# Combinations of x made earlier, one head's end of norm cut into eight pieces, another's moved forward

## The chip, the cores and the metric

The kernel runs on one core of a Trainium2 chip. The metric is the device time of one execution in microseconds. One core has five engines with a queue each: TensorE (PE, matmuls), VectorE (DVE), ScalarE (ACT), GpSimd (POOL) and SyncE (SP, which here only starts DMAs). Each engine works through its queue in order, and semaphores tie the queues together.

## The reference

One layer of a hybrid encoder, on 2048 new frames and 64 frames of a running stream. The core of it:

```python
p = rms_norm(x, norm_g) @ w_in            # aq, ak, av, ag, bq, bf, bi, bg, ma, mb
attn_o = window_attention(aq, ak, av)     # mixer A: window of two chunks of 64
# mixer B, for each chunk of 64 and each of 4 heads:
o = scores @ v + q_dec @ S                # read-out
S = exp(last) * S + k_end.T @ v           # update of the state
ya = (attn_o * silu(ag)) @ w_ba
rn = rec_o * rsqrt(mean(rec_o * rec_o) + EPS) * g_norm
yb = (rn * silu(bg)) @ w_bb
y = rms_norm(x + (sigmoid(ma) * ya + sigmoid(mb) * yb) @ w_o)
```

All arithmetic is to be as exact as float32: each matrix product is done in three passes over operands split into a high and a low part.

## The kernel before

The 2112 frames are cut into three groups of 704 columns (11 chunks of 64); each group runs the same stages. Within a group a projection of 128 output rows is two half blocks on PE, a first half of 320 columns and a second of 384, 24 matmuls each. `steps(g)` writes the order of one group as a list of steps, and each engine walks the same list and does its own part of each step. So a step's place in the list is its place in the queue of every engine that has a part in it. The order of a group:

- k, v and q of mixer A, then the projections of the four heads of mixer B (`bf`, `bq`, `bi`, `bg`), with attention in between. Behind each head's projections its recurrence runs beside the next head's; head 3's runs beside the gates of mixer A, `ag0` to `ag3`: `kend_t`, `v_t`, `scores_b` (masked scores, first half of ag1), `update` (second half of ag1), `read_out` (second half of ag2), `sum_sq` (second half of ag3).
- `update` on DVE (line 1204) adds the chunks' states one after the other and signals `last_made`; `read_out` on PE (line 1567 on) waits for it. ScalarE copies the read-out to `ob` and squares it, DVE makes the low part `sq_lo` (line 1226), PE sums the squares.
- `finish` (from line 1227, DVE alone) is the end of a head's norm: a reciprocal of 704 columns, two multiplications, a copy to the high part and a subtraction for the low part. ScalarE may copy the next head's read-out to `ob` only when it is done. Its signal `finished` is wanted by ScalarE's copy of the first product of the fourth pair, and by PE's `yb`.
- Most merge gates (`ma`, `mb`; 14 of 16 blocks) are computed in pairs by Strassen's scheme in Winograd's form: seven half-size products (`prod`, of 12 matmuls with 352 columns) instead of eight. That needs combinations of the two row halves and the two column halves of x. GpSimd makes two of the sums (line 650), `t_mix` on DVE two more sums and four differences, `t_high` (ScalarE) and `t_low` (DVE) split them, `t_last` and `t_low` 3 the last one, `t_one`, which is written over a quarter of x once the last full projection is through.
- The weights are combined too, in group 0 alone: `prep` makes the high part (ScalarE, line 701) and the sums (DVE, lines 1270 to 1283), `low` the low part (DVE, line 1046). Three of eight weight buffers hold the raw blocks of a pair (DMA, line 550), five are a ring for what is made. All that is made is kept in DRAM (`w_parts`, line 683) and groups 1 and 2 load it from there. A buffer may be made anew when PE has used it and its copy to DRAM has landed.
- In the products, line 1295 on DVE adds the products to each other out of their banks and frees these banks; line 929 on ScalarE copies the first one (`u_sum`), line 787 is ScalarE's sigmoid of the full gate projections.
- Then `ya`, `yb` (mixer outputs), `out` (output projection), norm of y, and x of the next group.

These lines of `steps` are the ones that the change touches:

```python
        if n == 4:
            out.append(("finish", B_HEADS - 2, 0))
    out.append(("t_mix", 0, 0))
...
        out += {1: [("t_high", 0, 0)], 2: [("t_high", 1, 0), ("t_high", 2, 0), ("t_low", 0, 0)]}.get(n, [])
        if n == 2 * len(firsts) - 2:
            out += prep(2, 3) + [("t_low", 1, 0), ("t_low", 2, 0)]
    out += [("t_last", 0, 0), ("prod", 0, 0)] + prep(4) + [("t_low", 3, 0), ("finish", B_HEADS - 1, 0)]
```

Of the kernel before, what the change touches and what calls it, by code (L numbers as in the profile page):

```python
# [12 lines left out]
F32 = mybir.dt.float32  # L13
# [4 lines left out]
ALU = mybir.AluOpType  # L18
# [16 lines left out]
B_HEADS = 4  # L35
# [4 lines left out]
T = NCH * CHUNK  # L40
# [113 lines left out]
def steps(g):  # L154

    last, out = g == GROUPS - 1, []

    def block(n):

        return [(kind, n, s) for s in range(2) for kind in ("proj", "evac")]  # L160


    hgrn = [["kend_t0", "kend_t1"], ["v_t0", "v_t1"], ["scores_b0", "scores_b1"], ["update0"],
            [], ["read_out0", "read_out1"], [], ["sum_sq0", "sum_sq1"]]

    def recurrence(n, h):
        return [(k[:-1], h, int(k[-1])) for k in hgrn[n]] if h >= 0 else []


    out += [(kind, n, s) for s in range(2) for n in ("ak", "av", "bf0") for kind in ("proj", "evac")]  # L170
    if g:
        out[4:4] = [("y_sum", 1, g - 1)]
        out[7:7] = [("y_back", 1, g - 1)]
    for n in ["aq0", "aq1"]:
        out += block(n)
    out += [("v_win", r, 0) for r in range(3)] + [("k_win", 0, 0)]
    for n in ["aq2", "aq3"]:
        out += block(n)
    heads = [(f"{n}{h}", s) for h in range(B_HEADS) for n in ("bf", "bq", "bi", "bg") for s in range(2)]
    for n, half in list(enumerate(heads))[2:]:  # L180


        h, i, k = n // 8, n % 8, (n - 2) // 2
        out.append(("proj", *half))
        chunk = [("attend", k - 2, 0)] if n % 2 else [("probs_t", k - 2, 0), ("scores", k, 0)]
        parts = [[t for t in chunk if 0 <= t[1] < NCH], [("evac", *half)], recurrence(i, h - 1)]
        order = {0: (2, 0, 1), 3: (0, 1, 2)}.get(i, (0, 2, 1))
        out += [t for j in order for t in parts[j]]
        if n % 2 == 0:
            out += [(kind, c, 0) for kind, c in (("softmax", k), ("normalise", k - 1)) if 0 <= c < NCH]  # L190
        if i == 4:
            out.append(("keys", h, 0))
        if i == 0 and h >= 2:
            out.append(("finish", h - 2, 0))
    gates = [(f"ag{j}", s) for j in range(A_GROUP) for s in range(2)]
    for n, half in enumerate(gates):

        parts = [("evac", *half)], recurrence(n, B_HEADS - 1)
        out += [("proj", *half)] + (parts[1] + parts[0] if n == 1 else parts[0] + parts[1])
        if n == 4:  # L200
            out.append(("finish", B_HEADS - 2, 0))
    out.append(("t_mix", 0, 0))

    def prep(*ops):
        return [("prep", n, 0) for n in ops if g == 0 and n < NO]

    firsts = PLAIN[NP - 2 * FIRST_PAIRS:]
    for n, half in enumerate((m, s) for m in firsts for s in range(2)):
        out += [("proj", *half), ("evac", *half)]
        if n == 2 * len(firsts) - 4:  # L210
            out += prep(0, 1)
        out += {1: [("t_high", 0, 0)], 2: [("t_high", 1, 0), ("t_high", 2, 0), ("t_low", 0, 0)]}.get(n, [])
        if n == 2 * len(firsts) - 2:
            out += prep(2, 3) + [("t_low", 1, 0), ("t_low", 2, 0)]
    out += [("t_last", 0, 0), ("prod", 0, 0)] + prep(4) + [("t_low", 3, 0), ("finish", B_HEADS - 1, 0)]
    for n in range(1, NO):
        out += ([("prod", n, 0)] + prep(n + AHEAD))[::1 if OPS[n][0] == "a11" else -1]
        out += {NO - 3: [("fetch", 0, 0)], NO - 1: [("fetch", 1, 0), ("refill", 0, 0)]}.get(n, [])
    for j in range(MERGES):
        out += [(n, j, s) for n in ("ya", "yb") for s in range(2)]  # L220
    for n, (j, s) in enumerate(OUT):
        if not last:
            out += X_STEPS.get(n, [])
        out.append(("out", j, s))
        if (j, s) == (KT - 3, 1):
            out += [("y_sum", 0, g), ("y_back", 0, g)]
    if last:
        out += [("y_sum", 1, g), ("y_back", 1, g)]
    if g == 0:
        out = [t for step in out for t in [step] + [("low", u, 0) for u in lows_after(step)]]  # L230
    return out
# [37 lines left out]
def program(nc, x_t, w, cache_k, cache_v, state, norm_gain, sinks, lb_logits, hgrn_gain, final_gain,  # L269
# [26 lines left out]
    gb_hi, at_gb_hi, _ = sb("gb_hi", [P, B_HEADS, T], F32R)  # L296
    ga_lo, at_ga_lo, _ = sb("ga_lo", [P, NCH, A_GROUP, CHUNK], F32R)
    gb_lo, at_gb_lo, _ = sb("gb_lo", [P, B_HEADS, T], F32R)
# [3 lines left out]
    gate_b = own("gate_b", [P, B_HEADS, T], F32, at_gb_lo)  # L302
# [3 lines left out]
    for h in range(HALVES):  # L306
# [15 lines left out]
    gain, gain_b = own("gain", [P, KT]), own("gain_b", [P, B_HEADS])  # L322
# [14 lines left out]
    f, at_f, _ = sb("f", [P, T + 1])  # L337
    prod = own("prod", [P, T])
    sq, at_sq, _ = sb("sq", [P, T])
    sq_lo = own("sq_lo", [P, T], F32R, at_sq)  # L340
    sq_hi, rs, ob = own("sq_hi", [P, T], F32R), own("rs", [P, T]), own("ob", [P, T])
    t_one = own("t_one", [P, 4, HT], F32, at_f)
# [28 lines left out]
    t_top = own("t_top", [P, 3, 4, HT], F32, at_t_hi)  # L371
    t_sum = own("t_sum", [P, 3, 4, HT], F32, at_t_lo)
# [25 lines left out]
    t_back, t_made, t_high, t_split, t_one_low = (sem("t_back"), sem("t_made"), sem("t_high"), sem("t_split"),  # L398
                                                  sem("t_one_low"))
# [3 lines left out]
    ob_copied, finished, gated_a = sem("ob_copied"), sem("finished"), sem("gated_a")  # L403
# [21 lines left out]
    def wait_read(eng, g, last, step, b):  # L425

        eng.wait_ge(read[b], START + use(g, last, step, b) + 1)

    def wait_block_read(eng, g, last, name):

        halves = [("proj", name, s) for s in range(2)]
        if bank_of(g, halves[0]) != bank_of(g, halves[1]):
            wait_read(eng, g, last, halves[0], bank_of(g, halves[0]))
        wait_read(eng, g, last, halves[1], bank_of(g, halves[1]))
# [531 lines left out]
    def _(dve):  # L966
        links = [0]

        def link(ins):

            links[0] += 1
            ins.then_inc(dve_step, 1)
            dve.wait_ge(dve_step, links[0])
# [74 lines left out]
        def split(hi, lo, val):  # L1048

            link(dve.tensor_copy(hi, val))  # L1050
            return dve.tensor_tensor(lo, val, hi.bitcast(F32), ALU.subtract)
# [18 lines left out]
        def body(g, last):  # L1070
            dve.sem_clear(dve_step)
            links[0] = 0
            for step in steps(g):
                kind, a, s = step
                if kind == "evac":
# [4 lines left out]
                    n = a[:2]  # L1080
# [17 lines left out]
                    elif n == "bf" and s == 1:  # L1098
                        h = int(a[2:])
# [10 lines left out]
                    elif n == "bq":  # L1110
                        h = int(a[2:])
                        wait_full(dve, g, last, step, bank)
                        dve.tensor_tensor(q_dec[:, h, lo:hi], src, prod[:, lo:hi], ALU.mult).then_inc(read[bank], 1)
                    elif n == "bg":
                        h = int(a[2:])
# [15 lines left out]
                elif kind == "keys":  # L1131

                    h = a
# [10 lines left out]
                elif kind == "scores":  # L1144
# [11 lines left out]
                    for b in (3, 4):  # L1156
# [5 lines left out]
                                                  in1=neg_sink[:], op0=ALU.mult, op1=ALU.min))  # L1162
# [9 lines left out]
                elif kind == "scores_b":  # L1172
                    h, b = a, banks(step)[0]
# [16 lines left out]
                elif kind == "update":  # L1190

                    h = a
# [5 lines left out]
                    for c in range(NCH):  # L1198
                        b = UPDATE_BANK[c]
                        i = UPDATE_BANKS[b].index(c)  # L1200
                        if i == 0:
# [3 lines left out]
                            out=dst, in0=st[:, c, :], scalar=decay[:, h, c:c + 1],  # L1205
                            in1=pb[b][:, i * P:(i + 1) * P], op0=ALU.mult, op1=ALU.add)
# [20 lines left out]
                elif kind == "finish":  # L1227
                    h = a
# [6 lines left out]
                                                  op0=ALU.mult, op1=ALU.mult))  # L1235
                    link(dve.tensor_tensor(ob[:], ob[:], gate_b[:, h, :], ALU.mult))
                    split(gb_hi[:, h, :], gb_lo[:, h, :], ob[:]).then_inc(finished, 1)
                elif kind == "t_mix":

                    def back(dst, k, t):  # L1240

                        v = slice(4 * k, 4 * k + 4), slice(HT * t, HT * t + HT)
                        return dve.tensor_tensor(dst, x_hi[:, v[0], v[1]].bitcast(F32),
                                                 x_lo[:, v[0], v[1]].bitcast(F32), ALU.add)

                    dve.wait_ge(t_back, 2 * g + 2)
                    back(t_sum[:, 1], 1, 0)
                    link(back(t_top[:, 1], 0, 0))
                    dve.tensor_tensor(t_one[:], t_top[:, 0], t_top[:, 1], ALU.subtract).then_inc(t_made, 1)
                    dve.tensor_tensor(t_sum[:, 0], t_sum[:, 2], t_top[:, 0], ALU.subtract).then_inc(t_made, 1)  # L1250
                    dve.wait_ge(t_made, 4 * g + 2)
                    dve.tensor_tensor(t_sum[:, 2], t_sum[:, 2], t_one[:], ALU.subtract).then_inc(t_made, 1)
                    dve.wait_ge(t_made, 4 * g + 3)
                    dve.tensor_tensor(t_sum[:, 1], t_sum[:, 1], t_sum[:, 2], ALU.subtract).then_inc(t_made, 1)
                elif kind == "t_low" and a == 3:
                    dve.wait_ge(t_high, 4 * g + 4)
                    dve.tensor_tensor(x_lo[:, 0:4, HT:T], t_one[:], x_hi[:, 0:4, HT:T].bitcast(F32),
# [5 lines left out]
                elif kind == "prep" and OPS[a][0] == "s3":  # L1263

                    n, at = a, PAIRS * g + OPS[a][1]
# [6 lines left out]
                elif kind == "prep" and OPS[a][0] == "s2":  # L1272
                    n, at = a, PAIRS * g + OPS[a][1]
# [61 lines left out]
                elif kind == "out":  # L1335
                    n = OUT.index((a, s))
# [362 lines left out]
```

## Time and profile before

| | us |
|---|---|
| median of three runs | 1567.97 |
| lowest and highest run | 1567.23, 1568.9 |
| profiled execution | 1567.78 |
| its span, first to last instruction | 1565.7 |
| group 0: first product | 308 |
| groups 1 and 2: head 3's read-out | 802.50, 1303.07 |

The mean granted clock of TensorE is 0.992 of full speed. The profile gives for each engine its instructions with start and duration in microseconds from the start of the span, and in brackets how long the engine stood idle before one and what ended that. Matmuls overlap in the rows, so their pace is read from start to start. Group 0 lasts until about 527 us, group 1 until about 1030.

### The profile page before, as it was taken

Reading aid. Unit: us, or ns where it says so; the run is one execution under the profiler, and the core shown is the slowest. Engines: PE = TensorE matmul, PEld = TensorE weight load, DVE = VectorE, ACT = ScalarE, POOL = GpSimd, SP = SyncE. Lnnn points to the kernel's source line nnn. Section 1 sums busy time; section 2 is a strip of 40 time slices with the busy share of each in tenths; the row PEclk is TensorE's granted clock in tenths of the full one; section 3 lists DMA queues with packets and bytes.
Section 4 is the critical chain, followed back from the end, with each engine's and each line's share of the span. In section 5 each row is a group of like instructions: output and inputs, shape, how many; then the busy total and the mean of one; then the engine's idle time right before and its main releaser. Section 6 shows DMA issues by size and latency. Waiting matters only on the chain.

```text
span 1565.7 us, 24417 instructions
## 1 busy us (share of the span) xinstructions
PE 1513.8 (97%) x9727; PEld 1459.3 (93%) x9727; DVE 967.2 (62%) x1658; ACT 552.4 (35%) x1193; POOL 40.0 (3%) x24
## 2 busy tenths in 40 slices
PE   6999999889999999999999999999999999999996
PEld 5998899888999999999999999999989999999996
DVE  5677877986676854677686136665566668414624
ACT  5355553434415522565222120531246423210022
POOL 2000001000001000000100000100000010000000
PEclk9999999999999999999999999999999999999998
DMA  4743344368896663222237884545332233886452
GB/s 158 281 169 125 136 151 158 124 251 305 322 329 231 229 233 117 108 85 96 100 112 229 275 291 172 209 145 202 111 112 82 85 112 111 270 273 203 138 200 74
DMA packets 99136, 278.44 MB, mean 178 GB/s; under 512 B 11984, under 2 KB 29136, under 8 KB 99024
## 3 DMA queue, kind: packets, MB, share of 16 engines
q1 hardware_dynamic: 73968, 202.68, 37.9%
q10 hardware_dynamic: 25056, 74.20, 12.2%
q8 instruction: 78, 1.28, 0.3%
q14 instruction: 34, 0.28, 0.1%
HBM read 194.01 MB, written 82.84 MB: 177 GB/s over the span
## 4 chain that ended last, share of the span: by engine, by line
PE 79%; DVE 11%; DMA 4%; ACT 3%; issue 2%; SPq 1%; ACTq 0%; DVEq 0%
PE bank L1366 23%; PE bank L1368 23%; PE bank L1367 23%; DMA w_parts<-w_unit 2%; PE bank L1571 2%; PE bank L1497 1%; DVE rs L1233 1%; PE bank L1567 1%; DMA raw<-in_w 1%; PE bank L1515 1%; DVE w_unit L1046 1%; PE bank L1529 1%; PE bank L1553 1%; PE bank L1539 1%; PE bank L1506 1%
## 5 line engine op out<-in xcount | busy, mean ns | idle before, releaser
L1366 PE MATMUL bank<-x_hi,w_unit 128*128 128x320 f32 (+2 forms) x1680 | 554.0, 330 | 22.0 <-DVE sig L1295 8.1
L1368 PE MATMUL bank<-x_hi,w_unit 128*128 128x320 f32 (+2 forms) x1680 | 543.6, 324 | 0.0
L1367 PE MATMUL bank<-x_lo,w_unit 128*128 128x320 f32 (+2 forms) x1680 | 543.3, 323 | 0.0
L1366 PEld LDWEIGHTS bank<-x_hi,w_unit 128*128 128x128 f32 x1680 | 317.3, 189 | 33.1 <-issue 18.8
L1367 PEld LDWEIGHTS bank<-x_lo,w_unit 128*128 128x128 f32 x1680 | 317.5, 189 | 0.4
L1368 PEld LDWEIGHTS bank<-x_hi,w_unit 128*128 128x128 f32 x1680 | 317.4, 189 | 0.0
L1366 PE MATMUL bank<-m_hi,w_unit 128*128 128x384 f32 (+1 forms) x384 | 125.7, 327 | 1.1 <-DVE w_unit L1046 1.1
L1368 PE MATMUL bank<-m_hi,w_unit 128*128 128x384 f32 (+1 forms) x384 | 123.8, 322 | 0.0
L1367 PE MATMUL bank<-m_lo,w_unit 128*128 128x384 f32 (+1 forms) x384 | 123.8, 322 | 0.0
L1366 PE MATMUL bank<-t_hi,w_unit 128*128 128x352 f32 x252 | 81.5, 324 | 0.0
L1367 PE MATMUL bank<-t_lo,w_unit 128*128 128x352 f32 x252 | 81.5, 323 | 0.0
L1368 PE MATMUL bank<-t_hi,w_unit 128*128 128x352 f32 x252 | 81.5, 323 | 0.0
L938 ACT ACTIVATE sig<-sig 128x352 f32<-128x352 f32 x63 | 31.1, 494 | 139.9 <-DVE sig L1295 139.9
L1046 DVE TENSOR_TENSOR w_unit<-w_raw,w_unit 128x512 fp32r<-128x512 f32 x96 | 65.0, 686 | 17.5 <-ACT w_unit L691 12.7
L1366 PEld LDWEIGHTS bank<-m_hi,w_unit 128*128 128x128 f32 x384 | 72.1, 188 | 2.2 <-issue 1.5
L1367 PEld LDWEIGHTS bank<-m_lo,w_unit 128*128 128x128 f32 x384 | 72.1, 188 | 0.7
L1368 PEld LDWEIGHTS bank<-m_hi,w_unit 128*128 128x128 f32 x384 | 72.1, 188 | 0.0
L691 ACT ACTIVATE w_unit<-w_raw 128x512 fp32r<-128x512 f32 x88 | 51.2, 624 | 47.3 <-DMA w_raw<-in_w 44.0
L1295 DVE TENSOR_TENSOR u_sum<-u_sum,bank 128x352 f32<-128x352 f32 x21 | 10.9, 520 | 90.1 <-PE bank L1368 90.1
L1342 DVE TENSOR_TENSOR res<-res,bank 128x320 f32<-128x320 f32 (+1 forms) x48 | 24.9, 518 | 65.5 <-PE bank L1368 62.4
L1366 PE MATMUL bank<-ga_hi,w_unit 128*128 128x320 f32 (+1 forms) x192 | 61.9, 323 | 0.9 <-DVE sig L1330 0.9
L1366 PE MATMUL bank<-gb_hi,w_unit 128*128 128x320 f32 (+1 forms) x192 | 62.0, 323 | 0.2 <-DVE sig L1330 0.2
(209 smaller groups left out, 2464.9 us busy)
## 6 DMA issues: line engine op xcount, KB each, us to landing
w_unit<-w_parts SPq DMA_DIRECT2D x274, 512.0 KB, 4.1
w_parts<-w_unit ACTq DMA_DIRECT2D x137, 512.0 KB, 4.3
w_raw<-in_w SPq DMA_DIRECT2D x88, 256.0 KB, 3.6
res<-in_x_t SPq DMA_DIRECT2D x12, 704.0 KB, 6.9
raw<-in_w SPq DMA_DIRECT2D x28, 256.0 KB, 5.4
x_raw<-in_x_t SPq DMA_DIRECT2D x12, 384.0 KB, 7.4
out_y<-res SPq DMA_DIRECT2D x12, 384.0 KB, 6.2
x_raw<-in_x_t SPq DMA_DIRECT2D x12, 320.0 KB, 5.6
```

The source lines that it names most:

```text
L691: act.activation(high_of(u), w_raw[PLACE[u]][:], ACT.Copy).then_inc(w_high, 1)
L938: act.activation(v, v, ACT.Sigmoid).then_inc(gates_made, 1)
L1046: dve.tensor_tensor(low_of(u), source, high_of(u).bitcast(F32), ALU.subtract).then_inc(w_split, 1)
L1233: link(dve.reciprocal(rs[:], rs[:]))
L1342: dve.tensor_tensor(r, r, pb[bank][:, 0:hi - lo], ALU.add).then_inc(read[bank], 1)
L1366: pe.matmul(out, w_h, m_h, start=first, stop=False, **more)
L1367: pe.matmul(out, w_h, m_l, start=False, stop=False, **more)
L1368: return pe.matmul(out, w_l, m_h, start=False, stop=last_of_bank, **more)
L1497: ins = pe.matmul(pb[3 + v][:, i * P:(i + 1) * P], q_rot[rows, c, 2 * i:2 * i + 2, :], k_rot[rows, c * CHUNK:c * CHUNK + P], start=True, s ...
L1506: ins = pe.transpose(pb[5][:, i * P:(i + 1) * P], probs[:, a % 2, i, :], ident[:])
L1515: ins = pe.matmul(pb[6][rows, 0:2 * P], v_win[:, a, rows], probs_t[:, 2 * v:2 * v + 2, :], start=True, stop=True)
L1571: ins = pe.matmul(pb[b][:, k * CHUNK:(k + 1) * CHUNK], st[:, c, :], q_dec[:, a, c * CHUNK:(c + 1) * CHUNK], start=False, stop=(c == chunks ...
```

## The change

- `t_mix` is cut into three steps. The first (two sums) comes behind head 3's first `bg` half, the second (two differences) behind its second half, the third (two more) behind the first half of ag0. Before, all six instructions came behind the last ag block.
- `finish` of head 2 moves from behind the first half of ag2 to behind the first half of ag1, behind `scores_b` and ahead of `update`.
- `t_high` 0 to 2 move into the last three ag halves; `t_low` 0 comes behind the first half of ma0, `t_low` 1 and 2 behind its second.
- `finish` of head 3 no longer comes in one piece behind the first product and `t_low` 3, but in eight (`finish_part`): four quarters of the reciprocal behind products 4, 6, 8 and 10, the two multiplications behind 12 and 14, the copy behind 16, the subtraction with the signal behind 18. The waits stand at the first piece.

```diff
--- before.py
+++ after.py
@@ -192,14 +192,19 @@
             out.append(("keys", h, 0))
         if i == 0 and h >= 2:
             out.append(("finish", h - 2, 0))
+        if h == B_HEADS - 1 and i in (6, 7):
+            out.append(("t_mix", i - 6, 0))
     gates = [(f"ag{j}", s) for j in range(A_GROUP) for s in range(2)]
     for n, half in enumerate(gates):
 
         parts = [("evac", *half)], recurrence(n, B_HEADS - 1)
         out += [("proj", *half)] + (parts[1] + parts[0] if n == 1 else parts[0] + parts[1])
-        if n == 4:
+        if n == 2:
             out.append(("finish", B_HEADS - 2, 0))
-    out.append(("t_mix", 0, 0))
+        if n == 0:
+            out.append(("t_mix", 2, 0))
+        if n >= 5:
+            out.append(("t_high", n - 5, 0))
 
     def prep(*ops):
         return [("prep", n, 0) for n in ops if g == 0 and n < NO]
@@ -209,12 +214,14 @@
         out += [("proj", *half), ("evac", *half)]
         if n == 2 * len(firsts) - 4:
             out += prep(0, 1)
-        out += {1: [("t_high", 0, 0)], 2: [("t_high", 1, 0), ("t_high", 2, 0), ("t_low", 0, 0)]}.get(n, [])
+        out += {0: [("t_low", 0, 0)], 1: [("t_low", 1, 0), ("t_low", 2, 0)]}.get(n, [])
         if n == 2 * len(firsts) - 2:
-            out += prep(2, 3) + [("t_low", 1, 0), ("t_low", 2, 0)]
-    out += [("t_last", 0, 0), ("prod", 0, 0)] + prep(4) + [("t_low", 3, 0), ("finish", B_HEADS - 1, 0)]
+            out += prep(2, 3)
+    out += [("t_last", 0, 0), ("prod", 0, 0)] + prep(4) + [("t_low", 3, 0)]
     for n in range(1, NO):
         out += ([("prod", n, 0)] + prep(n + AHEAD))[::1 if OPS[n][0] == "a11" else -1]
+        if n >= 4 and n % 2 == 0 and n < 20:
+            out.append(("finish_part", B_HEADS - 1, n // 2 - 2))
         out += {NO - 3: [("fetch", 0, 0)], NO - 1: [("fetch", 1, 0), ("refill", 0, 0)]}.get(n, [])
     for j in range(MERGES):
         out += [(n, j, s) for n in ("ya", "yb") for s in range(2)]
@@ -1235,6 +1242,25 @@
                                                   op0=ALU.mult, op1=ALU.mult))
                     link(dve.tensor_tensor(ob[:], ob[:], gate_b[:, h, :], ALU.mult))
                     split(gb_hi[:, h, :], gb_lo[:, h, :], ob[:]).then_inc(finished, 1)
+                elif kind == "finish_part":
+                    h, quarter = a, slice(T // 4 * (s % 4), T // 4 * (s % 4 + 1))
+                    if s == 0:
+                        wait_read(dve, g, last, ("sum_sq", h, 0), 7)
+                        wait_read(dve, g, last, ("sum_sq", h, 1), 5)
+                        dve.wait_ge(ob_copied, 2 * (B_HEADS * g + h + 1))
+                        wait_block_read(dve, g, last, f"bg{h}")
+                    if s < 4:
+                        link(dve.reciprocal(rs[:, quarter], rs[:, quarter]))
+                    elif s == 4:
+                        link(dve.scalar_tensor_tensor(out=ob[:], in0=ob[:], scalar=gain_b[:, h:h + 1], in1=rs[:],
+                                                      op0=ALU.mult, op1=ALU.mult))
+                    elif s == 5:
+                        link(dve.tensor_tensor(ob[:], ob[:], gate_b[:, h, :], ALU.mult))
+                    elif s == 6:
+                        link(dve.tensor_copy(gb_hi[:, h, :], ob[:]))
+                    else:
+                        dve.tensor_tensor(gb_lo[:, h, :], ob[:], gb_hi[:, h, :].bitcast(F32),
+                                          ALU.subtract).then_inc(finished, 1)
                 elif kind == "t_mix":
 
                     def back(dst, k, t):
@@ -1243,15 +1269,18 @@
                         return dve.tensor_tensor(dst, x_hi[:, v[0], v[1]].bitcast(F32),
                                                  x_lo[:, v[0], v[1]].bitcast(F32), ALU.add)
 
-                    dve.wait_ge(t_back, 2 * g + 2)
-                    back(t_sum[:, 1], 1, 0)
-                    link(back(t_top[:, 1], 0, 0))
-                    dve.tensor_tensor(t_one[:], t_top[:, 0], t_top[:, 1], ALU.subtract).then_inc(t_made, 1)
-                    dve.tensor_tensor(t_sum[:, 0], t_sum[:, 2], t_top[:, 0], ALU.subtract).then_inc(t_made, 1)
-                    dve.wait_ge(t_made, 4 * g + 2)
-                    dve.tensor_tensor(t_sum[:, 2], t_sum[:, 2], t_one[:], ALU.subtract).then_inc(t_made, 1)
-                    dve.wait_ge(t_made, 4 * g + 3)
-                    dve.tensor_tensor(t_sum[:, 1], t_sum[:, 1], t_sum[:, 2], ALU.subtract).then_inc(t_made, 1)
+                    if a == 0:
+                        dve.wait_ge(t_back, 2 * g + 2)
+                        back(t_sum[:, 1], 1, 0)
+                        link(back(t_top[:, 1], 0, 0))
+                    elif a == 1:
+                        dve.tensor_tensor(t_one[:], t_top[:, 0], t_top[:, 1], ALU.subtract).then_inc(t_made, 1)
+                        dve.tensor_tensor(t_sum[:, 0], t_sum[:, 2], t_top[:, 0], ALU.subtract).then_inc(t_made, 1)
+                    else:
+                        dve.wait_ge(t_made, 4 * g + 2)
+                        dve.tensor_tensor(t_sum[:, 2], t_sum[:, 2], t_one[:], ALU.subtract).then_inc(t_made, 1)
+                        dve.wait_ge(t_made, 4 * g + 3)
+                        dve.tensor_tensor(t_sum[:, 1], t_sum[:, 1], t_sum[:, 2], ALU.subtract).then_inc(t_made, 1)
                 elif kind == "t_low" and a == 3:
                     dve.wait_ge(t_high, 4 * g + 4)
                     dve.tensor_tensor(x_lo[:, 0:4, HT:T], t_one[:], x_hi[:, 0:4, HT:T].bitcast(F32),
```

## Rows read from the trace of the kernel before

**Rows 1.** The page, part 1: busy time, share of the span, number of instructions

```profile
PE 1513.8 (97%) x9727; PEld 1459.3 (93%) x9727; DVE 967.2 (62%) x1658; ACT 552.4 (35%) x1193; POOL 40.0 (3%) x24
```

**Rows 2.** Waits of PE, whole span: total us, times, longest us

```profile
PE bank L1366 <- DVE sig L1295: 8.1, 7, 2.0
...
PE bank L1366 <- ACT sig L787: 0.7, 1, 0.7
```

**Rows 3.** Timeline of DVE, group 1: start, duration, engine, line, [idle before <-releaser]

```profile
777.63 0.56 DVE L1117 TENSOR_TENSOR gate_b<-bank,gate_b 128x384 f32<-128x384 f32 x1 [6.50 <-ACT gate_b L821]
...
788.00 0.49 DVE L1124 TENSOR_TENSOR raw<-bank,raw 128x320 f32<-128x320 f32 x1 [0.74 <-ACT raw L829]
...
790.01 0.06 DVE L1182 MEMSET pad<- 128x1 f32 x1
...
793.81 0.56 DVE L1124 TENSOR_TENSOR raw<-bank,raw 128x384 f32<-128x384 f32 x1 [2.47 <-ACT raw L829]
...
795.87 0.22 DVE L1197 COPY st<-carry_s 128x128 f32<-128x128 f32 x1
...
800.56 0.35 DVE L1204 SCALAR_TENSOR_TENSOR carry_s<-st,decay,bank 128x128 f32<-128x128 f32 x1
...
803.03 4.55 DVE L1233 RECIPROCAL rs<-rs 128x704 f32<-128x704 f32 x1
...
810.90 0.55 DVE L1124 TENSOR_TENSOR raw<-bank,raw 128x384 f32<-128x384 f32 x1
...
821.54 1.62 DVE L1249 TENSOR_TENSOR t_one<-t_top 128x1408 f32<-128x1408 f32 x1
...
824.74 1.62 DVE L1252 TENSOR_TENSOR t_sum<-t_sum,t_one 128x1408 f32<-128x1408 f32 x1
```

**Rows 4.** Timeline of PE, group 1, head 3's read-out

```profile
802.50 1.05 PE L1567 MATMUL bank<-sc_t,v_tok 128*128 128x128 f32 x8
```

**Rows 5.** Timelines of DVE and of PE, group 0, around head 3's read-out

```profile
254.24 0.68 DVE L1046 TENSOR_TENSOR w_unit<-w_raw,w_unit 128x512 fp32r<-128x512 f32 x1
...
277.29 0.35 DVE L1204 SCALAR_TENSOR_TENSOR carry_s<-st,decay,bank 128x128 f32<-128x128 f32 x1
...
278.64 0.61 PE L1567 MATMUL bank<-sc_t,v_tok 128*128 128x128 f32 x4
...
291.82 0.50 PE L1582 MATMUL bank<-sq_hi,ones_r 128*128 128x512 f32 x1 [1.22 <-DVE sq_lo L1226]
```

**Rows 6.** Timeline of GpSimd (POOL), group 1

```profile
763.78 3.17 POOL L650 TENSOR_TENSOR t_top<-x_hi,x_lo 128x1408 f32<-128x1408 f32 x1
```

**Rows 7.** Timeline of PE, group 0, at the first products

```profile
313.87 0.40 PE L1366 MATMUL bank<-x_hi,w_unit 128*128 128x352 f32 x1 [3.76 <-ACT u_sum L929]
...
327.62 0.43 PE L1366 MATMUL bank<-x_hi,w_unit 128*128 128x352 f32 x1 [4.27 <-DVE w_unit L1046]
```

**Rows 8.** Stretches: length, busy PE, PEld, DVE, ACT, POOL; clock, DMA share, GB/s

```profile
314.00:318.00 4.00, 4.00 (x16) 4.00 (x17) 3.76 (x6) 0.93 (x2) 0.00 (x0) 0.57 0.02 4
...
378.00:383.00 5.00, 4.01 (x15) 4.04 (x16) 3.85 (x7) 1.89 (x4) 0.00 (x0) 0.66 0.65 260
383.00:398.00 15.00, 15.00 (x95) 15.00 (x94) 9.80 (x17) 6.17 (x12) 0.00 (x0) 1.00 0.85 316
833.00:930.00 97.00, 95.65 (x598) 95.14 (x597) 28.79 (x45) 16.96 (x35) 0.00 (x0) 1.00 0.84 272
```

**Rows 9.** One line by source: count, duration ns min/median/max

```profile
L1168 DVE RECIPROCAL rden<-rden x33: 177/178/180, 98.0 to 1237.4; 128x4 f32<-128x4 f32 x33
```

**Rows 10.** Timeline of DMA issues (SPq), and one piece of the chain, group 0

```profile
316.99 0.33 SPq L550 DMA_DIRECT2D raw<-in_w  x1
...
337.29 0.33 SPq L550 DMA_DIRECT2D raw<-in_w  x1
...
398.41 0.33 SPq L550 DMA_DIRECT2D raw<-in_w  x1
...
340.95 5.62 DMA w_parts<-w_unit
```

## The prediction

> **What bounds the kernel now.** I read the page first. TensorE (PE) is busy for 97% of the span, VectorE (DVE) for 62% [rows 1]. So time can only come out of PE's idle microseconds, or go into new ones. Next, the list of PE's waits: seven waits, 8.1 us, end with DVE's adds of line 1295, the longest 2.0 us; one of 0.7 us ends with line 787 [rows 2]. PE's timeline has two longer ones, 3.76 and 4.27 us, in group 0 close behind the start of the products [rows 7]. Groups 1 and 2 hold almost no waits. So only group 0 has anything large to give back.
>
> A wait of PE costs more than itself. Behind the one of 3.76 us PE starts 16 matmuls in 4 us at a granted clock of 0.57; elsewhere it starts 95 in 15 us at 1.00, one in 0.16 us [rows 8]. A granted clock of 0.57 is full speed (2.4 GHz) for a small part of the stretch and 1.2 GHz for the rest. 16 matmuls are worth 2.6 us, so 1.4 are lost, and by the clock (0.43 x 4) 1.7. I take 1.6. After the wait of 2.0 us, at 378 to 383 us, the clock is 0.66: the loss is the same.
>
> Then I read the queue of DVE, which works in order, from the last head's gate on. In group 1 it waits 6.50, 0.74 and 2.47 us among the gate blocks, then runs the update of head 3 until 800.91 [rows 3]. PE starts head 3's read-out at 802.50 [rows 4] and needs that update: 1.6 us to spare. In group 0 the update ends at 277.64 and the read-out starts at 278.64 [rows 5]: 1.0 us. This is the tight place, and the change puts work ahead of it.
>
> **Part 1: the combinations (t_mix) go forward.** The six instructions on 128x1408 stand in three pairs of 3.20 us from start to start (821.54 to 824.74) [rows 3]. The first pair now falls behind the gate of head 3's first half, inside the idle time of 6.50 us that begins at 771.1: free. GpSimd's two adds, for which it waits, end at 766.95 [rows 6]. The second pair stands behind the gate of the second half, which ends at 778.19, the third behind the first half of ag0: 6.4 us ahead of the update.
>
> **Part 2: head 2's end of norm** goes from behind the first half of ag2 to behind the first half of ag1, which is from behind the update to ahead of it. It takes 7.87 us (803.03 to 810.90) [rows 3]. Queued behind it are the second half of ag1 and the update, and so PE's read-out with every matmul after it.
>
> **The sum ahead of the read-out.** In group 1 DVE must do from 778.19 on, from start to start in rows 3: second pair 3.20, first half of ag0 2.01 (as 788.00 to 790.01), third pair 3.20, second half of ag0 2.06 (793.81 to 795.87), first half of ag1 2.01, masked scores 1.34 (790.01 to 791.34, where the wait of 2.47 begins), end of norm 7.87, second half of ag1 2.06, update 5.04 (795.87 to 800.91). That is 28.8 us, and all of it is ready when DVE gets there, so it ends at 807.0 against 802.5: PE waits **4.5 us**. Group 2 repeats these rows within 0.1 us: 4.5. In group 0 the start is 254.85 (0.61 behind 254.24) and four low parts of weights of 0.61 lie between: 31.2 us, so 286.0 against 278.64 [rows 5], **7.4 us**. Each is longer than 2.0 us, so 1.6 us for the clock go on each. Bounds of that: 0 (no row shows these short matmuls at the low clock) and 1.7; I take 1.6, since all waits of 2.0 us and more cost it.
>
> Given back: with its norm done early, head 2 no longer holds up ScalarE's copy of head 3's read-out, and PE's wait of 1.22 us for sq_lo goes in group 0 [rows 5]. In groups 1 and 2 PE did not wait there.
>
> **Part 3: t_high and t_low sooner.** They fit between the gate blocks on ScalarE, and behind them on DVE. That takes away the 0.7 us of group 1 at line 787 [rows 2], behind a ScalarE still busy with t_high. Of the 3.76 us in group 0 about 1.1 stay: the copy of t_one's high part must wait for the last full projection, and the first product's copy stands behind it.
>
> **Part 4: head 3's end of norm in eight pieces.** Before, these 7.87 us stood ahead of the low part for which PE waits 4.27 us [rows 7]. Now the pieces stand behind products 4, 6, ... 18. A quarter of the reciprocal is 4.55/4 = 1.14 us and a fixed part; a reciprocal of 4 elements takes 0.18 [rows 9], so about 1.3, and the other four are the old 3.3 us. In groups 1 and 2 DVE works 28.8 of 97 us there [rows 8], so they are free; without that cover they would cost up to 8.5 us. The Trainium skill (VectorE: DVE Perf Modes, "The TRN2 errata") speaks against cutting an instruction up, as each part pays a fixed latency again. The row of 4 elements agrees; it is 0.45 us for a reciprocal in four here, and is held in the sum already.
>
> **What comes next in group 0's products.** There a ring of five buffers sets the pace: each made weight is first written to DRAM, which takes up to 5.62 us, before its buffer is made anew. The raw weights of a pair are fetched when the last sum of the pair before is made. The fetches are issued at 316.99, 337.29, then 15.28 us apart on average until 398.41 [rows 10], while seven products take PE 7 x 12 x 0.16 = 13.4 us. So the change saves what it moves this chain forward against PE. The first product starts 12 x 0.16 us ahead of the wait of 3.76, at 308.1 [rows 7]; relative to it the fetches stood at 8.9, 29.2 and 90.3. Afterwards the first can come once the last full projection frees the ring, at 3.9: a copy, a low part and three sums of 0.6 to 0.8 us, with their waits. The second comes 15.3 later plus 2.0 for two pieces that stand directly between a low part and the sums of the next pair: 21.2. The last stands at 21.2 + 61.1 = 82.3. That is 8.0 us earlier, less 0.3 for later pieces: **7.7 us** won. Bounds: 2 (all the pieces lie in the chain) and 17 (the chain never binds: all waits but 1.1 go, 3.76 + 4.27 + the 6.7 of line 1295's 8.1 us that lie in group 0, and 3.2 of lowered clock).
>
> **Total.** Group 0: 7.4 + 1.6 - 1.2 - 7.7 = +0.1. Group 1: 4.5 + 1.6 - 0.7 = +5.4. Group 2: 4.5 + 1.6 = +6.1. Sum +11.6. The profiled execution took 1567.8 us (span 1565.7), 0.2 under the median of the runs, so 1579.4 in all.
>
> **The rivals.**
> *A, the forecast*: the update is late in all three groups, 1579.4. For it speaks that the durations repeat from group to group and that nothing in that queue waits.
> *B, the weak form*: the stalls come, but the clock stays up behind them (-4.8) and the chain gives 11 instead of 7.7: 1571.3. Or the clock falls and all 17 us come back: 1570.1, the border to no change. For it: the wait of 1.22 us cost no more than itself. Against: 2.0 us and more did. The Trainium skill (TensorE: Matmul & The Clock Gate, Part 1) ties the clock to recent activity; by that rule all three stalls would lower it, as in A.
> *C, faster*: head 2's end of norm fits ahead of the update after all. The point that decides is whether DVE ends the update before PE is through the second half of ag2, that is whether 28.8 us of work shrink to 24.3 in group 1, and 31.2 to 23.8 in group 0. Then only gains stay, 1.2 + 0.7 + 7.7: 1558.2. The steadiness of the rows speaks against it.
> *D, the pieces cost more*: all of them lengthen group 0's chain, 5.7 us more: 1585.1. For it: DVE works 9.8 of 15 us there [rows 8], and each piece stands directly ahead of a low part or a sum.
> *E, it does not come sooner*: the first pair waits for GpSimd, and all behind it slips. GpSimd is done 4.2 us before [rows 6]; only what it is late beyond that counts. It ends slower too.
>
> **How the numbers follow.** A 0.70, B 0.12, C 0.06, D 0.10, E 0.02. The range is 1571 (B) to 1585 (D); it leaves out C and the edge of B. Two measurements of this kernel tell apart about 0.2%, 3.1 us. Faster by more: C and a little, 0.07. Within: the edge of B, 0.06. Slower: the rest, 0.87.
>
> **What would show it.** Right: PE idle 4 to 5 us ahead of line 1567 at the last head of groups 1 and 2 and 6 to 7 in group 0, ended by DVE's line 1204; DVE without a gap from head 3's gate to the end of the update; a granted clock under 0.7 right behind; the wait of 4.27 us gone and 1 us left of the 3.76; the fetches of raw weights about 8 us earlier relative to the first product; no wait for sq_lo. Wrong: gaps in DVE's queue ahead of the update, no wait at line 1567, or more waits at the products of group 0 than before. The dearest error would be in the sum ahead of the read-out, since it enters three times.

## The result, and the profile after

| | before | changed |
|---|---|---|
| median of four runs, us | 1568.08 | 1591.49 |
| lowest and highest | 1567.23, 1568.9 | 1589.92, 1593.45 |
| profiled execution, us | 1567.78 | 1591.22 |
| its span, us | 1565.7 | 1589.2 |
| mean granted clock | 0.992 | 0.982 |

The ratio is 1.015, with a 95% interval of 1.0132 to 1.0168: 23.4 us slower. The forecast was 1579.4, 11.6 us slower, with a range that ended at 1585, so the measured time lies beyond it. The direction was right, the size only half.

The page of the changed kernel, part 1, against [rows 1]:

```profile
PE 1527.6 (96%) x9727; PEld 1472.7 (93%) x9727; DVE 967.0 (61%) x1667; ACT 552.8 (35%) x1193; POOL 40.1 (3%) x24
```

PE is busy for 13.8 us more than before with the same 9727 matmuls, so they ran longer. That is already a sign that waits are not all. PE's waits, whole span (against [rows 2]; line 1596 is the old 1567, line 1324 the old 1295):

```profile
PE bank L1596 <- DVEq L1224: 14.4, 3, 6.1
PE bank L1395 <- DVE sig L1324: 10.9, 9, 2.8
...
PE bank L1395 <- ACT u_sum L936: 2.2, 3, 0.9
PE bank L1582 <- DVE sc_t L1195: 1.5, 2, 1.1
```

There is one new entry: three waits, 14.4 us in all, at the first matmul of head 3's read-out. The profile puts them down to line 1224 of DVE's queue, the signal behind the update. They are 6.06 us in group 0 and 4.19 in groups 1 and 2. DVE's timeline of group 1, against [rows 3]:

```profile
783.41 0.56 DVE L1124 TENSOR_TENSOR gate_b<-bank,gate_b 128x384 f32<-128x384 f32 x1 [3.50 <-ACT gate_b L828]
783.89 1.61 DVE L1277 TENSOR_TENSOR t_one<-t_top 128x1408 f32<-128x1408 f32 x1
...
786.95 0.48 DVE L1131 TENSOR_TENSOR raw<-bank,raw 128x320 f32<-128x320 f32 x1
...
797.42 4.54 DVE L1240 RECIPROCAL rs<-rs 128x704 f32<-128x704 f32 x1
...
805.28 0.55 DVE L1131 TENSOR_TENSOR raw<-bank,raw 128x384 f32<-128x384 f32 x1
...
807.33 0.22 DVE L1204 COPY st<-carry_s 128x128 f32<-128x128 f32 x1
...
812.02 0.35 DVE L1211 SCALAR_TENSOR_TENSOR carry_s<-st,decay,bank 128x128 f32<-128x128 f32 x1
...
822.05 0.89 DVE L1233 TENSOR_TENSOR sq_lo<-sq,sq_hi 128x704 fp32r<-128x704 f32 x1 [5.42 <-ACT sq_hi L906]
```

After 3.50 us of idle time nothing in this queue waits until the last row: second pair of combinations, first half of ag0, third pair, the next two halves, end of norm from 797.42, second half of ag1 from 805.28, update from 807.33 to 812.37. That is 28.4 us behind the gate (783.97). The sum of 28.8 holds. PE's timeline right behind, against [rows 4]:

```profile
812.57 2.05 PE L1596 MATMUL bank<-sc_t,v_tok 128*128 128x128 f32 x8 [4.19 <-DVEq L1224]
...
820.30 0.61 PE L1395 MATMUL bank<-x_hi,w_unit 128*128 128x320 f32 x1
820.71 0.47 PE L1396 MATMUL bank<-x_lo,w_unit 128*128 128x320 f32 x1
...
823.91 0.47 PE L1396 MATMUL bank<-x_lo,w_unit 128*128 128x320 f32 x1
...
824.41 0.31 PE L1395 MATMUL bank<-x_hi,w_unit 128*128 128x320 f32 x1
...
846.79 0.40 PE L1395 MATMUL bank<-x_hi,w_unit 128*128 128x352 f32 x1 [0.67 <-ACT sig L794]
```

The last of these rows is the first product. In the kernel before it stands here:

```profile
831.49 0.40 PE L1366 MATMUL bank<-x_hi,w_unit 128*128 128x352 f32 x1 [0.67 <-ACT sig L787]
```

And the stretches around it, with the columns of [rows 8]: length, busy PE, PEld, DVE, ACT, POOL, then the granted clock, DMA share, GB/s:

```profile
812.00:816.00 4.00, 3.43 (x16) 3.46 (x17) 3.67 (x8) 0.00 (x0) 0.00 (x0) 0.50 0.21 75
816.00:820.00 4.00, 4.00 (x19) 3.66 (x18) 0.59 (x2) 1.09 (x2) 0.00 (x0) 0.50 0.00 0
820.00:824.00 4.00, 4.00 (x17) 4.00 (x17) 0.89 (x1) 2.61 (x4) 0.00 (x0) 0.50 0.00 0
824.00:828.00 4.00, 4.00 (x26) 4.00 (x25) 1.49 (x4) 1.71 (x2) 0.00 (x0) 0.95 0.00 0
```

This is what the forecast did not have. The read-out took 4.05 us before (802.50 to 806.55); it takes 7.73 now (812.57 to 820.30), all at 1.2 GHz, and the projection behind it starts its matmuls 0.27 us apart until 824.2; at full speed they start 0.15 us apart. From the start of the read-out to the first product, which waits for the sigmoid of the last full projection, PE needed 28.99 us before (802.50 to 831.49) and 34.22 now (812.57 to 846.79): **5.2 us** for the clock, not 1.6. In the same way it is 4.5 us in group 2 and, with the old wait of 1.2 us for sq_lo left out, 5.4 in group 0.

### The profile page after: what moved, and what is told of

It is laid out like the page before. It is cut to its first block, busy times and chain, and to the rows that moved or that the text cites. A ratio compares the mean times of both kernels' runs of the same rounds, so it can differ in the third digit from the quotient of the medians.

```text
span 1589.2 us, 24440 instructions
## 1 busy us (share of the span) xinstructions
PE 1527.6 (96%) x9727; PEld 1472.7 (93%) x9727; DVE 967.0 (61%) x1667; ACT 552.8 (35%) x1193; POOL 40.1 (3%) x24
## 4 chain that ended last, share of the span: by engine, by line
PE 78%; DVE 12%; DMA 5%; ACT 3%; issue 2%; SPq 0%; ACTq 0%; DVEq 0%
PE bank L1395 23%; PE bank L1397 22%; PE bank L1396 22%; DMA w_parts<-w_unit 2%; PE bank L1600 2%; PE bank L1596 2%; DMA raw<-in_w 1%; PE bank L1526 1%; PE bank L1544 1%; DVE rs L1240 1%; PE bank L1535 1%; PE bank L1558 1%; DVE w_unit L1053 1%; PE bank L1582 1%; DVE st L1211 1%
```

## The experiments

Each is one kernel compared with the kernel before on the same chip. "Waits" are PE's, from its list of waits.

**1. Undo one part: head 2's end of norm back behind the update.**

```diff
-        if n == 2:
+        if n == 4:
             out.append(("finish", B_HEADS - 2, 0))
```

> The changed kernel with one part undone: head 2's end of norm stands behind the first half of ag2 again, behind the update. Theory: all of the loss comes from that one place. In group 1 DVE has 13.8 us of work between the gate of head 3 (778.2 in the kernel before) and the second half of ag1, which is ready at 793.8 anyway, so the update ends as before and PE does not wait at the read-out; in group 0 it ends 0.6 us later than before, inside the 1.0 us to spare. What stays is the gain at group 0's products, 6 to 8 us: about 1561 us. Rival: the early combinations or the pieces cost something themselves; then it stays above the kernel before, 1568 or more.

Measured: 1562.06 us, ratio 0.9959 (0.9944 to 0.9974). No wait at the read-out in any group, and the clock stays up there. This kernel is 7.1 us faster than the kernel before where the changed one is 23.4 slower: this one line costs some 30 us, and the rest of the change taken together is a gain.

**2. The same part alone, on the kernel before.**

```diff
-        if n == 4:
+        if n == 2:
             out.append(("finish", B_HEADS - 2, 0))
```

> The kernel before with one part of the change alone: head 2's end of norm ahead of the update. From the rows of before, the update ends 5.0 us after PE wants it in group 0 and 3.8 us in groups 1 and 2, together 12.6 us; the wait of 1.2 us for sq_lo goes. Theory (the low clock behind such a stall lasts 9 to 13 us, because the short matmuls of the read-out follow it): another 14 to 19 us, so 1593 to 1598 in all. Rival (the low clock costs 1.6 us a stall as behind the waits at the products): 1584.

Measured: 1593.86 us, ratio 1.016 (1.0145 to 1.0175). The waits at the read-out are 4.91, 3.73 and 3.73 us, within 0.1 us of the sum from rows of before, 12.4 in all. Read from the start of the read-out to the first product, as above, the clock costs 5.5, 4.5 and 5.9 us, 15.8 in all in the profiled execution. Group 1, the end of the wait and the stretches behind it:

```profile
816.07 2.04 PE L1567 MATMUL bank<-sc_t,v_tok 128*128 128x128 f32 x8 [3.73 <-DVEq L1217]
...
816.00:820.00 4.00, 3.93 (x19) 3.96 (x19) 3.78 (x8) 0.00 (x0) 0.00 (x0) 0.50 0.19 68
820.00:824.00 4.00, 4.00 (x18) 3.66 (x18) 0.12 (x1) 1.08 (x2) 0.00 (x0) 0.50 0.00 0
824.00:828.00 4.00, 4.00 (x22) 4.00 (x22) 0.89 (x1) 1.34 (x3) 0.00 (x0) 0.73 0.00 0
```

**3. A stall as long, with long matmuls behind it.** The kernel before, with one wait more on PE:

```diff
                     lo, hi = sub(s)
+                    if (kind, a, s) == ("proj", "ag3", 0):
+                        pe.wait_ge(finished, START + B_HEADS * g + 3)
                     wait_bank_free(pe, g, last, step, bank)
```

> The kernel before with one wait added: PE waits ahead of the first half of ag3, a block of 24 long matmuls, until head 2's end of norm is done. By the rows of before that is a stall of 5.6 us in group 0 and of 4.4 us in groups 1 and 2, as long as those of the changed kernel, but with long matmuls behind it instead of the read-out. Theory (what PE does behind the stall sets how long the clock stays low): low for about 3.5 us, 1.6 us a stall; 14.4 + 4.8 - 1.2, so 1586 us. Rival (the length of the stall sets it): low for 9 to 13 us here too, 1597 us.

Measured: 1584.93 us, ratio 1.0103 (1.0088 to 1.0119), 15.8 us slower. The waits are 5.49, 4.29 and 4.29 us, 14.1 in all, and 1.2 at sq_lo is gone. Group 1, where PE starts again, and the stretches behind it:

```profile
816.79 0.63 PE L1366 MATMUL bank<-x_hi,w_unit 128*128 128x320 f32 x1 [4.29 <-DVE gb_lo L1051]
...
816.00:820.00 4.00, 3.21 (x12) 3.21 (x13) 3.40 (x6) 2.32 (x5) 0.00 (x0) 0.50 0.00 0
820.00:824.00 4.00, 4.00 (x23) 4.00 (x22) 0.94 (x3) 0.44 (x1) 0.00 (x0) 0.81 0.00 0
824.00:828.00 4.00, 4.00 (x26) 3.92 (x25) 1.74 (x4) 1.10 (x2) 0.00 (x0) 1.00 0.03 4
```

The clock is up again within 5 us of the restart in all three groups. From the restart to the first product it costs 1.2, 1.9 and 1.1 us, for stalls about as long as those of the changed kernel. The length of the stall is not what keeps it down.

**4. The read-out one half block later.**

```diff
-            [], ["read_out0", "read_out1"], [], ["sum_sq0", "sum_sq1"]]
+            [], [], ["read_out0", "read_out1"], ["sum_sq0", "sum_sq1"]]
```

> The changed kernel with the read-out of each head one half block later, behind the first half of ag3 (for the other heads behind the first half of their bg block), so that PE reaches it 3.6 us later. Theory: the stalls of 4.2 us in groups 1 and 2 shrink to about 0.5 and leave the clock alone; in group 0 about 2.6 of the 6.1 us stay, and with it perhaps the low clock: 1563 to 1571 us. Rival: the later read-out only moves the stall to the sum of squares, 4 us a group again: above 1580 us.

Measured: 1569.06 us, ratio 1.0006 (0.9995 to 1.0017). The waits shrink to 2.56, 0.68 and 0.67 us. It is not the remedy, since the later read-out adds some 2.5 us of waits at the other heads of group 0. But its ten runs fall into two kinds: seven between 1567.7 and 1569.6 us with a mean clock of 0.992 to 0.994, three between 1573.7 and 1574.2 with 0.990 and 0.991. The profiled run is one of the three. Group 0, the wait and the stretches behind it, and one stretch of group 1:

```profile
289.95 2.05 PE L1596 MATMUL bank<-sc_t,v_tok 128*128 128x128 f32 x8 [2.56 <-DVEq L1224]
...
290.00:294.00 4.00, 4.00 (x19) 4.00 (x20) 3.83 (x8) 0.44 (x1) 0.00 (x0) 0.50 0.15 61
...
298.00:302.00 4.00, 4.00 (x14) 4.00 (x14) 0.89 (x1) 2.57 (x4) 0.00 (x0) 0.50 0.01 2
302.00:306.00 4.00, 4.00 (x23) 3.92 (x23) 0.84 (x2) 1.38 (x2) 0.00 (x0) 0.87 0.07 15
810.00:814.00 4.00, 3.32 (x28) 3.09 (x27) 3.61 (x10) 0.07 (x1) 0.00 (x0) 1.00 0.40 161
```

Behind 2.56 us the clock is at 1.2 GHz until about 303; behind 0.68 us in group 1 it never falls. A wait of 2.56 us is in the range in which the clock falls in some cases and not in others (see the last section): I read the two kinds of runs as the clock falling there in some and not in others. The profile shows only one kind, so that is argued, not shown.

**5. The same stall at the same place, long matmuls first.** As experiment 4, but PE waits for the update already ahead of the first half of ag3:

```diff
+                    if (kind, a, s) == ("proj", "ag3", 0):
+                        pe.wait_ge(last_made, START + B_HEADS * (g + 1))
                     wait_bank_free(pe, g, last, step, bank)
```

> As the kernel with the later read-out, but PE waits for the update already ahead of the first half of ag3. So PE stands still at the place, for the reason and as long as in the changed kernel (6.1, 4.2 and 4.2 us); only what follows differs: 24 long matmuls of the projection first, then the read-out. Theory (what PE does behind the stall sets how long the clock stays low): low for 3.5 to 4 us instead of 13.7, 13.5 and 9.5, so about 12.6 us less than the changed kernel, 1579 us. Rival (the read-out keeps the clock low wherever it comes, or the length of the stall sets it): 1588 to 1592 us.

Measured: 1583.83 us, ratio 1.0105 (1.0089 to 1.012). That is 7.7 us under the changed kernel, with nearly the same waits (5.91, 4.03, 4.04) and 2.5 us more of waits at the other heads, so some 10 us come from the clock. The 1579 were too low, as I had left those other waits out and had put the clock's part at 12.6 us; the rival's 1588 were not reached. Group 1, PE's timeline and the stretches:

```profile
811.99 0.41 PE L1395 MATMUL bank<-x_hi,w_unit 128*128 128x320 f32 x1 [4.03 <-DVE carry_s L1211]
...
812.57 0.47 PE L1395 MATMUL bank<-x_hi,w_unit 128*128 128x320 f32 x1
...
815.76 0.37 PE L1395 MATMUL bank<-x_hi,w_unit 128*128 128x320 f32 x1
...
842.35 0.40 PE L1395 MATMUL bank<-x_hi,w_unit 128*128 128x352 f32 x1 [0.67 <-ACT sig L794]
```

```profile
807.00:811.00 4.00, 0.96 (x6) 0.64 (x4) 3.56 (x12) 1.75 (x2) 0.00 (x0) 1.00 0.49 181
811.00:815.00 4.00, 3.01 (x13) 3.01 (x14) 3.65 (x9) 0.00 (x0) 0.00 (x0) 0.68 0.20 83
815.00:819.00 4.00, 4.00 (x31) 4.00 (x30) 2.25 (x6) 0.44 (x1) 0.00 (x0) 0.89 0.11 33
819.00:823.00 4.00, 4.00 (x29) 3.81 (x29) 0.95 (x3) 2.58 (x6) 0.00 (x0) 1.00 0.00 0
```

Matmuls are 0.27 us apart from 812.57 to 815.76, 3.2 us, then the clock is up, and the read-out behind runs at full speed. From the restart to the first product PE needs 30.36 us (811.99 to 842.35) for the same work as the 34.22 of the changed kernel and the 28.99 of before. The clock costs 1.4 us here and 5.2 there. With 1.2 and 2.2 us in groups 2 and 0 against 4.5 and 5.4, this is the cleanest pair: same cause, same stall, other order behind it. What it does not separate is which property of the read-out keeps the clock low: its matmuls have 64 to 128 columns against 320 and 384, and each is one pass over plain float32 operands, where the projection makes three passes over split ones (lines 1395 to 1397). Once the clock is up, the read-out (4.05 us) does not bring it down.

**6. How early is too early.** Head 2's end of norm directly behind the update (`n == 3`):

> The changed kernel with head 2's end of norm one half block later: behind the second half of ag1, directly behind the update instead of ahead of it. Theory: what counts is the order of these two in DVE's queue; the update then ends in time, no wait at the read-out, and the time is that of the kernel with the end of norm one block later still, 1561 to 1563 us. Rival: the earlier place itself is what hurts, in proportion to how early; then half of the loss stays, about 1577 us.

Measured: 1561.01 us, ratio 0.996 (0.9945 to 0.9975). Only the order of the two in DVE's queue counts.

**7. and 8. The two gains apart.** The kernel before with the eight pieces alone, and with the combinations, t_high and t_low alone; in both, the other parts are as before.

> The kernel before with head 3's end of norm in eight pieces and nothing else. Theory: the wait of 4.3 us for a low part goes and its low clock (1.6 us) too, the wait of 3.8 for the copy of the first product stays. The fetches of raw weights decide: the first still 8.9 us behind the first product, the second 17.3 later instead of 20.3; so about 3 us are won, 1565 us. Rival: the two parts of the change at the products are worth the same 7 us each, whichever comes first, since the chain makes up the rest: 1561.

> The kernel before with the combinations, t_high and t_low made early and nothing else; head 3's end of norm is whole again behind the first product. Theory: the first fetch comes 3.6 us behind the first product instead of 8.9, the second still 20.3 later, as the 7.9 us on DVE stay in between: 5 us won, 1562 to 1563 us. Rival: the end of norm then stands directly before low parts that PE wants sooner, and the wait of 4.3 us for one grows to what was saved: 1566 to 1568.

Measured: the pieces alone 1566.63 us, ratio 0.9995 (0.9986 to 1.0004), no gain that can be told, against 1565 and the rival's 1561; the combinations alone 1562.55, ratio 0.997 (0.996 to 0.9981). In the first, the wait of 3.77 us stays, the one of 4.3 goes, and the waits for line 1295's adds grow to 8.5 us between 335 and 450 us (before, 6.7). Its fetches stand at 316.8 and 334.1, 17.3 us apart as forecast, but of the gain of 3 us only 2.2 are left at the last wait of the products in the profiled execution, one of the fastest of the eleven, and 0.7 in the median. In the second a wait of 3.52 us for the low part is left. Experiment 6 has both and ran on the same chip: its four runs (1560.22 to 1561.13) all lie under the seven of the combinations alone (1561.98 to 1563.64), so at these places the pieces add some 1.5 us.

**9. The pieces moved into DVE's gaps**, on the kernel of experiment 1:

```diff
-        if n >= 4 and n % 2 == 0 and n < 20:
-            out.append(("finish_part", B_HEADS - 1, n // 2 - 2))
+        at = {1: [0], 2: [1], 3: [2], 8: [3], 9: [4], 15: [5, 6], 16: [7]}
+        out += [("finish_part", B_HEADS - 1, q) for q in at.get(n, [])]
```

> The changed kernel with head 2's end of norm behind the update again, and head 3's pieces moved to where DVE stands idle in group 0: behind products 1, 2, 3, 8, 9, 15 (two) and 16. Theory: the two pieces that stand between a low part and the sums of the next pair cost 2 to 2.5 us of the chain; out of its way, the second fetch comes 15.3 instead of 17.6 us behind the first, and the time falls to 1559 to 1560 us. Rival: the chain waits for transfers anyway, and nothing changes: 1562.

Measured: 1558.55 us, ratio 0.9944 (0.9932 to 0.9957). The kernel of experiment 1, DVE in group 0: a quarter of the reciprocal (line 1253) stands between a low part and the first sum of the next pair.

```profile
326.20 0.69 DVE L1053 TENSOR_TENSOR w_unit<-raw,w_unit 128x512 fp32r<-128x512 f32 x1 [0.57 <-ACT w_unit L708]
326.81 1.25 DVE L1253 RECIPROCAL rs<-rs 128x176 f32<-128x176 f32 x1
328.09 0.69 DVE L1306 TENSOR_TENSOR raw<-raw 128x512 f32<-128x512 f32 x1
```

The kernel with the pieces moved: the sum follows at once, and the second fetch (SPq rows) comes 16.0 us behind the first, not 17.6:

```profile
324.79 0.69 DVE L1053 TENSOR_TENSOR w_unit<-raw,w_unit 128x512 fp32r<-128x512 f32 x1 [0.56 <-ACT w_unit L708]
325.40 0.68 DVE L1306 TENSOR_TENSOR raw<-raw 128x512 f32<-128x512 f32 x1
...
311.78 0.33 SPq L557 DMA_DIRECT2D raw<-in_w  x1
...
327.74 0.33 SPq L557 DMA_DIRECT2D raw<-in_w  x1
```

In the profiled execution the clock stays at full speed through all the products. That is not where the gain comes from: the five runs have mean clocks from 0.993 to 0.996 and lie within 0.8 us. The gain over experiment 6, on the same chip, is 2.5 us; the second fetch came 0.7 us later than the 15.3 forecast.

**10. Both improvements** (`n == 3`, pieces in the gaps):

> The kernel with the pieces in DVE's gaps, and head 2's end of norm directly behind the update instead of one half block later. Theory: PE's wait for sq_lo in group 0 is 0.4 or 0.6 us either way and nothing else waits for the norm, so the time is the same, 1558 to 1559 us. Rival: ScalarE's copy of the read-out comes 2.6 us sooner and takes a wait away: 1557.

Measured: 1558.72 us, ratio 0.9941 (0.9929 to 0.9954): the same as experiment 9.

## Why the prediction was half right

- *The tight place*: right. The sum ahead of the read-out gave 4.5, 4.5 and 7.4 us; measured are 4.19, 4.19 and 6.06 + 1.09 = 7.15 (the 1.09 stand a little earlier, at PE's matmuls of the update, where experiment 1 has them too; the forecast did not part the two). Experiment 1 shows that this place is the whole loss.
- *The clock behind the stalls*: this term failed. It was taken as 1.6 us each, with 1.7 as its upper bound, from rows behind waits at the products, where 24 and more long matmuls follow. It measured 5.4, 5.2 and 4.5 us: 15.1 in all instead of 4.8. The three stalls stand ahead of the read-out, whose 34 matmuls have 64 to 128 columns. These alone take 3.7 us more at 1.2 GHz (7.73 instead of 4.05), and the clock comes back only 2.5 to 4.4 us into the projection that follows. Experiments 3 and 5 show that it is this order: with the projection first, stalls as long cost 1.1 to 2.2 us. The bound was no bound: no row showed short matmuls behind a stall, so it had to reach at least to the read-out's own length at half speed (4.05 us) plus the 1.6 of before, 5.7. With that, the upper end would have been 1597.
- *Group 0's products*: 7.7 us were forecast. The fetches of raw weights (SPq) of the changed kernel:

```profile
323.94 0.33 SPq L557 DMA_DIRECT2D raw<-in_w  x1
...
341.52 0.33 SPq L557 DMA_DIRECT2D raw<-in_w  x1
...
404.12 0.33 SPq L557 DMA_DIRECT2D raw<-in_w  x1
```

  Relative to the start of its first product (320.14) they stand at 3.8, 21.4 and 84.0; forecast were 3.9, 21.2 and 82.3. From the first product to the last wait at line 1295's adds (421.40 before, 427.29 now) PE takes 107.2 us instead of 113.4: 6.2 us won. That the chain binds held. The two pieces cost it about what was forecast: 1.6 us went when experiment 9 moved them. From the second fetch to the last it takes 62.6 us, not 61.1, so the later pieces cost more than the 0.3 I gave them.
- *The 0.7 us at line 787*: did not go. The first product of group 1 waits for the sigmoid of the last full projection. In both kernels that sigmoid starts as soon as the projection's last matmul ends (830.82 and 830.86 before, 846.12 and 846.16 now), with t_high just ahead of it or without, so t_high did not stand in the way. Of the 3.76 us at the copy of the first product 0.89 are left (forecast 1.1), and the 1.2 at sq_lo went.
- *The account*: 7.15 + 5.4 - 1.2 - 6.2 in group 0, 4.2 + 5.2 in group 1, 4.2 + 4.5 in group 2: 23.3 us, against a difference of the spans of 23.5.
- *The rivals*: C did not come, B neither. D's way was right, its cause small: the later pieces cost a little more than forecast, not 5.7 us. The early combinations alone are a gain (experiment 8), so E fell too.

## What to carry to other kernels

When a step is moved ahead in an in-order queue, add up everything between it and the next thing another engine waits for; here the sum from rows was right to 0.3 us, and one half block decided between 0.4% faster and 1.5% slower. A stall of the matmul engine must be priced by what stands behind it: here the read-out's 34 short matmuls ran at half speed from first to last, while the block of long matmuls won the clock back in 3 to 5.4 us. If a stall can't be avoided, put a dense block between it and the short work.

## What the runs showed of the hardware

- Behind the stalls of 3.7 to 6.1 us ahead of the read-out or the projection the granted clock is 0.50. With long matmuls behind (320 columns, experiments 3 and 5) it rose again 3.0 to 5.4 us after the restart. With the read-out's short ones behind (the changed kernel and experiment 2) it stayed at 0.50 for all of their 7.7 us and for 2.4 to 5.5 us of long matmuls more, 10 to 13 us in all. How the chip judges that, the runs don't tell.
- There is no sharp edge in the length of a wait. In group 0's products and at the read-out, over all the profiled executions, no wait of 1.0 to 1.8 us was followed by 1.2 GHz, and every one of 3.2 us and more was. In between it went both ways: the clock fell behind waits of 1.99 us (the stretch from 378 us in [rows 8]) and of 2.31, and stayed up behind 2.33 (the pieces alone), 2.73 (experiment 6), 2.75 (experiment 4) and 2.88 us (experiment 9):

```profile
370.24 0.40 PE L1395 MATMUL bank<-x_hi,w_unit 128*128 128x352 f32 x1 [2.88 <-DVE sig L1324]
370.00:374.00 4.00, 3.76 (x24) 3.79 (x25) 2.85 (x6) 1.67 (x4) 0.00 (x0) 1.00 0.68 268
```

  So the prediction's reading that every wait of 2.0 us and more costs the clock held in its own trace and not in all.
- A reciprocal of 176 columns takes 1.25 us, one of 704 columns 4.55: four quarters cost 0.45 us more than the whole.
